# Merged tiles rounded by ScalarE, the marks moved out of one attention step, and other banks for the first pool gate

## The reference, cut to what matters

```
gates  = sigmoid(g_pre + b_gate)                     # three gates per token and feature
merged = gates[0] * (y_a @ w_branch[0])              # mLSTM branch
       + gates[1] * (y_b @ w_branch[1])              # sparse attention branch, top-k mask by an indexer
       + gates[2] * (y_c @ w_branch[2])              # differential attention branch
x = x + merged @ w_out
x = x + (silu(g) * u) @ w_down                       # feed-forward, after a norm
```

## Time and profile before

| what | us |
|---|---|
| median of 3 runs (range) | 3100.09 (3099.02 to 3102.33) |
| the profiled execution | 3097.38 |
| its span | 3095.6 |
| PE busy | 2990.5 |
| POOL busy | 1992.7 |
| DVE busy | 1483.7 |
| ACT busy | 639.6 |

### The profile page before, as it was taken

How to read it: one execution, slowest core, us unless ns; L and a number is a source line. 1 busy time by engine, 2 the same in 40 slices (tenths; PEclk the granted TensorE clock), 3 DMA queues, 4 the chain that set the end, 5 groups by cost and what they waited for, 6 DMA issues and landing times.

```text
span 3095.6 us, 37945 instructions
## 1 busy us (share of the span) xinstructions
PE 2990.5 (97%) x14046; PEld 2450.7 (79%) x14046; DVE 1483.7 (48%) x2413; ACT 639.6 (21%) x1420; POOL 1992.7 (64%) x2041
## 2 busy tenths in 40 slices
PE   8989999999999998999999999999999999999998
PEld 6877778788888877778788888778878888888886
DVE  6678784633324777875643322465321221224543
ACT  3255332100001336433110000000111111211000
POOL 6755544777777766444677777687776555555775
PEclk9999999999999999999999999999999999999999
DMA  4322222333334322222333333233333223222332
GB/s 147 97 68 69 63 68 59 125 95 95 94 94 127 95 82 79 63 61 62 113 93 97 95 94 104 80 91 109 93 91 102 75 77 95 79 82 70 95 96 74
DMA packets 87068, 274.66 MB, mean 89 GB/s; under 512 B 10384, under 2 KB 11025, under 8 KB 86929
## 3 DMA queue, kind: packets, MB, share of 16 engines
q1 hardware_dynamic: 85392, 270.71, 28.8%
q10 hardware_dynamic: 1536, 2.10, 0.3%
HBM read 266.48 MB, written 4.19 MB: 87 GB/s over the span
## 4 chain that ended last, share of the span: by engine, by line
PE 88%; DVE 8%; ACT 2%; issue 1%; POOL 0%; DMA 0%; SPq 0%; DVEq 0%; ACTq 0%; POOLq 0%
PE PS L483 58%; PE PS L532 13%; PE PS L762 5%; PE PS L770 3%; PE PS L833 2%; PE PS L810 1%; PE PS L821 1%; PE PS L1056 1%; PE PS L496 1%; ACT TB L1166 1%; PE PS L1031 0%; DVE SMALLS L1674 0%; PE PS L1023 0%; DVE MSK L1975 0%; DVE SQ L1706 0%
## 5 line engine op out<-in xcount | busy, mean ns | idle before, releaser
L453 POOL TENSOR_TENSOR WL<-RAW,WH 128x512 fp32r<-128x512 f32 (+2 forms) x538 | 795.5, 1479 | 9.8
L445 POOL TENSOR_TENSOR POOL_C<-POOL_C 128x1 f32<-128x1 f32 x538 | 128.6, 239 | 1033.3 <-PE PS L483 593.6
L483 PE MATMUL PS<-XNH,WH 128*128 128x512 f32 x1752 | 692.7, 395 | 6.1 <-DVE EA L2127 3.0
L483 PE MATMUL PS<-XNL,WH 128*128 128x512 f32 x1752 | 683.4, 390 | 0.0
L450 POOL TENSOR_TENSOR WL<-RAW,WH 128x512 fp32r<-128x512 f32 x420 | 579.8, 1380 | 35.0
L446 POOL TENSOR_SCALAR WH<-RAW 128x1024 fp32r<-128x1024 f32 (+3 forms) x538 | 527.5, 980 | 0.6 <-issue 0.3
L483 PE MATMUL PS<-XNH,WL 128*128 128x512 f32 x1752 | 434.3, 390 | 0.1
L483 PEld LDWEIGHTS PS<-XNH,WH 128*128 128x128 f32 x1752 | 328.9, 188 | 79.8 <-issue 7.9
L483 PEld LDWEIGHTS PS<-XNL,WH 128*128 128x128 f32 x1752 | 328.9, 188 | 70.8 <-issue 2.9
L483 PEld LDWEIGHTS PS<-XNH,WL 128*128 128x128 f32 x1752 | 327.4, 187 | 69.8 <-POOL WL L453 1.0
L532 PE MATMUL PS<-WH,XNH 128*128 128x512 f32 x704 | 279.1, 396 | 6.9 <-ACT VEXT L1166 2.9
(11 more groups left out here) (372 smaller groups left out, 4558.8 us busy)
## 6 DMA issues: line engine op xcount, KB each, us to landing
RAW<-w_oslot SPq DMA_DIRECT2D x56, 512.0 KB, 3.6
RAW<-w_L0ffn SPq DMA_DIRECT2D x44, 512.0 KB, 3.6
RAW<-w_L1ffn SPq DMA_DIRECT2D x44, 512.0 KB, 3.6
RAW<-w_od SPq DMA_DIRECT2D x32, 512.0 KB, 3.6
RAW<-w_L0G SPq DMA_DIRECT2D x24, 512.0 KB, 3.6
RAW<-w_L1G SPq DMA_DIRECT2D x24, 512.0 KB, 3.6
RAW<-w_epg SPq DMA_DIRECT2D x16, 512.0 KB, 3.6
RAW<-w_eug SPq DMA_DIRECT2D x16, 512.0 KB, 3.6
```

The costliest lines, as they stand in the source:

```text
L445: nc.gpsimd.tensor_tensor(POOL_C[:, 1:2], POOL_C[:, 0:1], POOL_C[:, 0:1], ALU.add)
L453: nc.gpsimd.tensor_tensor(WL[:, half, at_:w], RAW[:, slot, at_:w], WH[:, half, at_:w].bitcast(F32), ALU.subtract).then_inc(S("weights_spli ...
L483: mm = nc.tensor.matmul(bank, w[:, slot, k * cols:(k + 1) * cols], x[:, k0 + k, :], start=first and j == 0 and w is WH and x is hi, stop=l ...
```

## The change

It has four parts.

1. For tiles 16 to 23, DVE adds the last contribution into merged(dt) in place; ACT makes MH from it by a copy with rounding (without the factor one half); DVE makes the low part in a function of its own, merged_low, which is issued one turn of the loop later (for the last tile, behind the loop). The products of branches 16 to 23 go by turns to the two halves of TMP.
2. The factor one half is put into the residual addition, which becomes a scalar_tensor_tensor in updates 0 and 2.
3. MARKS: the first step of the second attention has no marks (it had 3); the third after it has 5 (4), the next two 4 each (3).
4. The gate products of the first pool group go to banks 2 and 3, not 0 and 1.

```diff
+        def gate_count(g):
+            return g + 1 if g < 18 else 20 + 2 * (g - 18)
+        def high_count(i):
+            return 19 + 2 * i if i < 6 else 25 + i
+        def used_count(g):
+            return g + 1 if g < 16 else 17 + 2 * (g - 16)
...
-                    claim(t)
-                    by_columns(PS[t][:, :], c + t, (c + t) % 2, KD, XNH, XNL)
-                    release[t] = (S("e_gs"), 2 * g + t + 1)
+                    b = t if g else 2 + t
+                    claim(b)
+                    by_columns(PS[b][:, :], c + t, (c + t) % 2, KD, XNH, XNL)
+                    release[b] = (S("e_gs"), 2 * g + t + 1)
...
-                for i in range(2, 8):
-                    gate(16 + i)
+                for i in range(8):
+                    dt = LATE_FIRST[i]
+                    act.wait_ge(*L("gate_used", 18 + 2 * i))
+                    run(MH[:, dt, :], merged(dt), ACT.Copy, L("gate_ready"))
+                    if i < 6:
+                        gate(18 + i)
...
+                    if update in (0, 2):
+                        V.scalar_tensor_tensor(x_, more, 0.5, x_, ALU.mult, ALU.add).then_inc(S("x_updated"), 1)
...
-                    dst = merged(dt) if g < 8 else TMP[:, 0, :]
+                    dst = merged(dt) if g < 8 else TMP[:, g % 2 if g > 15 else 0, :]
...
-                        then(V.tensor_tensor(TMP[:, 1, :], merged(dt), TMP[:, 0, :], ALU.add))
-                        then(V.tensor_scalar(MH[:, dt, :], TMP[:, 1, :], 0.5, 0.0, ALU.mult, ALU.add))
-                        V.scalar_tensor_tensor(ML[:, dt, :], TMP[:, 1, :], 0.5, MH[:, dt, :].bitcast(F32),
-                                               ALU.mult, ALU.subtract).then_inc(L("merged_ready"), 1)
+                        V.tensor_tensor(merged(dt), merged(dt), dst, ALU.add
+                                        ).then_inc(L("gate_used"), 1)
+
+                def merged_low(g):
+                    dt = LATE_FIRST[g - 16]
+                    dve.wait_ge(*L("gate_ready", high_count(g - 16)))
+                    V.tensor_tensor(ML[:, dt, :], merged(dt), MH[:, dt, :].bitcast(F32), ALU.subtract
+                                    ).then_inc(L("merged_ready"), 1)
...
-                MARKS = (0, 0, 5, 10, 14, 18, 22, 25, 28, 31, 34, 38, 42, 45, 48)
+                MARKS = (0, 0, 5, 10, 14, 18, 22, 25, 28, 28, 31, 35, 40, 44, 48)
...
                     use_gate(16 + i)
                     if i < 6:
                         scale_gate(18 + i)
+                    if i:
+                        merged_low(15 + i)
+                merged_low(23)
```

More of the change, by code:

```diff
@@ L49 @@
     squared=28, square_used=28, hall_ready=16, k_scaled=64, rk_ready=2, root_taken=7, att_s=64, att_max=64, att_neg=16, att_e=32, att_p=48, att_t=48,
-    att_pt=48, att_o=48, att_y=8, y_tm=1, ya_low=4, yc_low=4, yb_low=4, gate_ready=24, gate_used=24,
+    att_pt=48, att_o=48, att_y=8, y_tm=1, ya_low=4, yc_low=4, yb_low=4, gate_ready=32, gate_used=32,
     merged_ready=8, silu_ready=22, hidden_used=22, hidden_ready=22,
@@ L781, in branch @@
                                ready=None if g % 8 else lambda k: L(low, k + 1), midway=midway)
-                    release[b] = L("gate_used", g + 1)
+                    release[b] = L("gate_used", used_count(g))
                 for half in range(2):
@@ L1624, in add_residual @@
                         x_, more = by_class(x_), heads(more, 4)
-                    V.tensor_tensor(x_, x_, more, ALU.add).then_inc(S("x_updated"), 1)
+                    if update in (0, 2):
+                        V.scalar_tensor_tensor(x_, more, 0.5, x_, ALU.mult, ALU.add).then_inc(S("x_updated"), 1)
+                    else:
+                        V.tensor_tensor(x_, x_, more, ALU.add).then_inc(S("x_updated"), 1)
                     if v == 6:
@@ L1982, in use_gate @@
                     more = PS[branch_bank(g)][:, :]
-                    dve.wait_ge(*L("gate_ready", g + 1))
+                    dve.wait_ge(*L("gate_ready", gate_count(g)))
                     dve.wait_ge(S("chunk_done"), seg(f"B{g}") + 1)
-                    dst = merged(dt) if g < 8 else TMP[:, 0, :]
+                    dst = merged(dt) if g < 8 else TMP[:, g % 2 if g > 15 else 0, :]
                     V.scalar_tensor_tensor(dst, SG[g % 2], 1.0, more, ALU.add, ALU.mult
                                            ).then_inc(L("gate_used"), 1)
-                    dve.wait_ge(*L("gate_used", g + 1))
+                    dve.wait_ge(*L("gate_used", used_count(g)))
                     if 8 <= g < 16:
@@ L2151, in _ @@
                     dve.wait_ge(S("chunk_done"), FIRST[f"epg{g}"] + t + 1)
-                    V.tensor_tensor(GA[:, t, :], PS[t][:, :], RT[:, :], ALU.mult
+                    V.tensor_tensor(GA[:, t, :], PS[t if g else 2 + t][:, :], RT[:, :], ALU.mult
                                     ).then_inc(S("e_gs"), 1)
```

## The result

| | us, median (range, runs) | to the kernel before (95% interval) |
|---|---|---|
| before | 3100.68 (3099.02 to 3102.33, 4) | |
| changed | 3080.55 (3079.05 to 3083.25, 4) | 0.9936 (0.9925 to 0.9948) |

The changed kernel is 20.1 us faster (16.1 to 23.3). The forecast was 12.8, the range ended at 3083.5. The sign and the three places were right; the terms for the marks and for the merged tiles were too small.

The account below looks back on a forecast made before the run. The prediction took PE to bound the kernel (busy 97% of the span), so only its waits could be won. Marks 4.2 + pool gate 4.6 + merged tiles 4.0 = 12.8 us; 3100.1 - 12.8 = 3087.3, range 3083.5 to 3092.5.

Parts of the forecast that it names:

- The three places: Marks in the second attention, first pool gate, and merged tiles at w_out: 4.2, 4.6 and 4.0 us faster.
- The marks: Second attention, both layers: PE's 2.01 us wait for TB goes, 2.1 per layer, 4.2 us in all; bounds 3.0 and 4.3.
- DVE's lateness at step 4: Second attention: after the fifth mark DVE starts step 4's maxima 0.3 to 0.4 us late, with about 1 us of cover.
- The clock held through it ..., so there is no more to win: Second attention: clock granted 1.00 behind the marks' wait, so the gain stays at 2.1 us per layer.
- The pool gate: Pool stage, first gate tile: without the bank conflict the step falls from 10.98 to 6.34, 4.6 us; bounds 3.0 and 4.7.
- The merged tiles: w_out in both layers: shorter waits for the last ML, 4.0 us together; bounds 1.0 and 11.
- The order of DVE's work: Last two branches before w_out: multiply and add of 22, low of 21, multiply and add of 23, lows of 22, 23.
- The w_out chunks: Weight loads for w_out: first chunk lands at 561.7, POOL wants it at 562.84; hidden. Late chunks were a rival, 0.04.
- ML's 1.66 with POOL busy beside it is the nearest row and the upper bound: Low parts before w_out: each taken at 1.66 us, lower bound 0.69, giving PE waits of 1.6 and 1.1.
- I take one of the two layers with each: w_out: clock holds in one layer (2.85 us won), falls in the other (1.2), 4.0 together.
- The first rival: Clock holds at every place, w_out included: 14.5 us faster, time 3085.6; chance 0.2.
- The upper bounds of the three terms: Largest gains allowed: marks 4.3, pool gate 4.7, merged tiles 11 us (0.69 for each low part).

Follow-up runs that it names:

- b4_one_op: The changed kernel with one more DVE operation (128x512 multiply of two SBUF tiles) ahead of the last two low parts; 3086.55 us (0.9960).
- The second and third profile: Two more profiles of the kernel before, without an edit; they took 3100.76 and 3099.90 us, where the first profile took 3097.38.

## Why the prediction was wrong

- **The marks.** The wait of 2.01 went and nothing came back; DVE's lateness at step 4 came as forecast and was covered. The step that failed is "The clock held through it ..., so there is no more to win". It held in that one execution. In the five profiles with this wait the clock fell behind it in 6 of 10 passages, 1.6 us each. The term is 4.5 to 7.7 by the profiles, 5.3 (2.5 to 8.1) by the runs, not 4.2.
- **The pool gate.** Right for its profile: 4.6. In the other profiles with that wait it cost 4.9 to 6.1; the runs say 3.1 (0.3 to 5.9).
- **The merged tiles.** The order of DVE's work was right, row for row. The w_out chunks were in time as forecast: POOL took the first at 561.36, 0.19 behind DVE's multiply of the same branch (0.20 before), and PE did not wait for it. Mis-sized was the low part: "ML's 1.66 with POOL busy beside it is the nearest row and the upper bound". I took that value for all three. But the 1.66 was 1.11 left of POOL's subtraction and 0.55 more, and belongs to that place only; it is no upper bound either. The trace of the kernel before held another price too: the ML at 527.08 took 0.69. The first took 1.78, the last two 0.68 and 1.36. That made the waits 0.5 and 0.7, so the second half of the step failed too, "I take one of the two layers with each": the clock held in both. 7.9 in place of 4.0.
- **The clock's rule.** The prediction set waits of 3.84 and 3.03, behind which it fell, against 2.01, behind which it held, and looked for the new waits between them. The same trace has the 3.53 at 1179.25 behind which it held. The first rival had the clock right but for waits that did not occur; b4_one_op suggests that at waits near the forecast's the clock falls (1.95 and 0.64, 1.95 and 0.95).
- **The base.** I forecast from the median, 2.7 us above the profiled execution, and priced the waits in that execution. The second and third profile, 3.4 and 2.5 us longer, show what such a distance is made of: 3.1 us of clock behind the marks' waits, 1.6 behind the wait at 1179, less 2.0 of shorter waits, and up to 0.6 at each of a few places elsewhere. The change removes only the first.
- **The range.** The upper bounds of the three terms, 4.3, 4.7 and 11, add up to 20.0, a time of 3080.1, which is where the result lies. The stated range left that out.

Against the first profile the measured terms add up to 17.0, against the two others to 20.4 and 20.5, and the medians differ by 20.1. That these lie so near is partly luck, as the intervals of the parts are 5.6 us wide and other places of the program give or take up to 3.5 us from one execution to the next.

## What to carry to other kernels

Behind waits of TensorE of 1.2 to 3.5 us the clock fell here in some executions and held in others, and the length did not say in which: take more than one profile before you price it, and ask what the profiled execution's distance from the median is made of. Here one more operation of 0.7 us on VectorE cost four times itself, 2.8 us per layer. Before you carry the duration of a VectorE operation from one place to another, look at what GpSimd is in the middle of at both. Where an engine waits for the last tile of a product, let it do the low products of the tiles it has first: by the profile that took the whole wait out; the run times could not tell it.

## What the runs showed of the hardware

The same VectorE subtraction of two 128x512 SBUF tiles took 0.68 to 1.78 us in one kernel: 0.69 when GpSimd was between two operations, and otherwise the rest of GpSimd's operation and 0.54, in 182 of 182 cases, whatever its form. Where VectorE started first, GpSimd was stretched: its subtraction took 1.83 in place of 1.29. And TensorE's clock behind one and the same wait fell in some executions and held in others: behind 2.0 us in 6 of 10 passages.
